# The first part's square sums at the end of a feed-forward block, moved beside the block's last products

## What is computed

```python
f1 = swiglu(rms_norm(x, ffn1_pre_g[l]), ffn1_w_gate[l], ffn1_w_up[l], ffn1_w_down[l])
x = x + FFN_RESIDUAL_WEIGHT * rms_norm(f1, ffn1_post_g[l])
m = token_mixer(rms_norm(x, mix_pre_g[l]), w_in[l], ...)
...
f2 = swiglu(rms_norm(x, ffn2_pre_g[l]), ffn2_w_gate[l], ffn2_w_up[l], ffn2_w_down[l])
x = x + FFN_RESIDUAL_WEIGHT * rms_norm(f2, ffn2_post_g[l])
```

## Time and profile before

| | us |
|---|---|
| median of 3 runs | 4127.95 |
| lowest, highest run | 4118.88, 4129.35 |
| the profiled execution's own time | 4127.35 |
| its span, first to last instruction | 4125.6 |
| PE busy in the span | 3960.3 |
| DVE busy | 1906.0 |
| ACT busy, POOL busy | 1408.2, 1416.1 |

### The profile page before, as it was taken

The page is one execution under the profiler, slowest core; times in us unless marked ns, Lnnn a source line. Parts: engine busy times, 40 slices in busy tenths (PEclk is TensorE's granted clock), DMA queues, the critical chain, the costliest instruction groups (busy, mean ns, idle before and its releaser), DMA issues.

```text
span 4125.6 us, 49381 instructions
## 1 busy us (share of the span) xinstructions
PE 3960.3 (96%) x20616; PEld 3199.7 (78%) x20616; DVE 1906.0 (46%) x2819; ACT 1408.2 (34%) x2256; POOL 1416.1 (34%) x849
## 2 busy tenths in 40 slices
PE   7999999999999999999999999999988999999988
PEld 5888888666565556888888789999967998888867
DVE  3323223533344535232232477654387526666654
ACT  3111111433333334111111354331253336666663
POOL 2222323133443452223232224432262123434364
PEclk9999999999999999999999999999999999999989
DMA  2111111110000021111111101121112220000014
GB/s 93 51 41 51 52 41 57 61 43 21 21 21 21 16 83 56 42 51 52 41 57 46 36 31 42 52 98 50 61 36 82 95 62 28 26 28 28 23 63 136
DMA packets 57807, 206.08 MB, mean 50 GB/s; under 512 B 7344, under 2 KB 10992, under 8 KB 57200
## 3 DMA queue, kind: packets, MB, share of 16 engines
q1 hardware_dynamic: 45744, 158.55, 11.7%
q0 software_dynamic: 9280, 41.75, 2.7%
q10 hardware_dynamic: 2560, 2.61, 0.2%
HBM read 177.40 MB, written 25.49 MB: 49 GB/s over the span
## 4 chain that ended last, share of the span: by engine, by line
PE 78%; DVE 12%; ACT 4%; POOL 3%; issue 1%; DMA 0%; DVEq 0%; ACTq 0%
PE ps L395 15%; PE ps L396 15%; PE ps L397 15%; PE ps L3509 4%; PE ps L3441 2%; PE ps L3443 2%; PE ps L3442 2%; PE ps L1354 2%; PE ps L1356 2%; PE ps L1355 2%; PE ps L3493 2%; POOL wlo L369 2%; PE ps L3539 2%; PE ps L546 2%; PE ps L1454 2%; PE ps L1425 1%
## 5 line engine op out<-in xcount | busy, mean ns | idle before, releaser
L369 POOL TENSOR_TENSOR wlo<-raw,whi 128x1024 fp32r<-128x1024 f32 x286 | 690.1, 2423 | 832.5 <-ACT whi L360 832.2
L395 PE MATMUL ps<-fxh,whi 128*128 128x512 f32 x1488 | 605.1, 407 | 41.6 <-POOL wlo L369 19.3
L396 PE MATMUL ps<-fxh,wlo 128*128 128x512 f32 x1488 | 582.1, 391 | 0.0
L397 PE MATMUL ps<-fxl,whi 128*128 128x512 f32 x1488 | 581.2, 391 | 0.0
L395 PE MATMUL ps<-xh,whi 128*128 128x352 f32 (+1 forms) x1400 | 473.5, 338 | 11.8 <-DVE sxin L2662 5.1
L396 PE MATMUL ps<-xh,wlo 128*128 128x352 f32 (+1 forms) x1400 | 450.7, 322 | 0.0
L397 PE MATMUL ps<-xl,whi 128*128 128x352 f32 (+1 forms) x1400 | 450.0, 321 | 0.0
L360 ACT ACTIVATE whi<-raw 128x1024 fp32r<-128x1024 f32 x286 | 294.8, 1049 | 451.9 <-PE ps L397 383.5
L395 PEld LDWEIGHTS ps<-fxh,whi 128*128 128x128 f32 x1488 | 280.7, 189 | 121.2 <-issue 35.8
L805 POOL TENSOR_TENSOR hl<-t,hh 128x512 fp32r<-128x512 f32 x88 | 114.0, 1295 | 733.1 <-ACT hh L750 733.1
L396 PEld LDWEIGHTS ps<-fxh,wlo 128*128 128x128 f32 x1488 | 280.9, 189 | 67.9 <-issue 12.1
(11 more groups left out here) (424 smaller groups left out, 7812.1 us busy)
## 6 DMA issues: line engine op xcount, KB each, us to landing
raw<-in_w_dram SPq DMA_DIRECT2D x286, 512.0 KB, 3.3
rs_scratch<-res POOLq DMA_DIRECT2D x2, 4160.0 KB, 14.0
res<-rs_scratch POOLq DMA_DIRECT2D x8, 520.0 KB, 5.1
szin<-zs_scratch SPq DMA_DIRECT2D x8, 520.0 KB, 3.2
gs_scratch<-oot POOLq DMA_DIRECT2D x8, 520.0 KB, 5.9
res<-rs_scratch POOLq DMA_DIRECT2D x2, 1408.0 KB, 6.7
og<-gs_scratch POOLq DMA_DIRECT2D x16, 176.0 KB, 2.6
oot<-rs_scratch POOLq DMA_DIRECT2D x2, 1408.0 KB, 9.1
```

What stands on the lines that cost most here:

```text
L369: pool.x.tensor_tensor(K.wlo[n % 3][:, :], K.raw[n % 2][:, :], K.whi[n % 3][:, :], ALU.subtract).then_inc(*S.up("w_lo", n))
L395: pe.x.matmul(out, wh, xh, start=k == 0, stop=False)
L396: pe.x.matmul(out, wl, xh, start=False, stop=False)
L397: last = pe.x.matmul(out, wh, xl, start=False, stop=k == K - 1)
```

## The change

At both ends the stage 0 squares of part a are summed behind groups 2 to 7 of the first pass (rows 0 to 5, in a new method `ahead`) and behind groups 0 and 1 of the second (rows 6 and 7), one at a time. DVE takes a's mean at group 1 of the second pass and its root at group 3, and applies rows 0 to 3 beside groups 4 to 7, with the rests of rows 0 to 2. Of part b's squares PE sums five behind the pass and the other three within the next product, behind rows 1 to 3. ACT's order follows: b's last three squares stand between a's rounded rows, and the next weight unit is rounded behind a's row 3 rather than ahead of row 0. Part b's mean and root stand at a's rows 5 and 7 on DVE rather than at 3 and 5. The arithmetic is the same.

```diff
-def pe_paced(pe, L, st):
+def pe_paced(pe, L, st, other=None):
     def wait(k):
         pe.wait_ge("late_lo", (L.tag, k))
         if st and k:
             pe_square(pe, L, 1, k - 1)
+            if other and k < 4:
+                pe_square(pe, other, 0, k + 4)
@@ pe_ffn
         down_group(10, 0, ft, wh, wl)
+        after.ahead(ft)
@@ new
+def act_two_norms(act, a, b, unit):
+    for k in range(8):
+        act_square(act, a, 0, k)
+        if k == 3:
+            act_units(act, unit)
+    act_root(act, a, 0)
+    for k in range(5):
+        act_square(act, b, 0, k)
+    for k in range(8):
+        act_high(act, a, k)
+        act_square(act, a, 1, k)
+        if k < 3:
+            act_square(act, b, 0, k + 5)
+        if k == 3:
+            act_units(act, unit + 1)
+        if k == 5:
+            act_root(act, b, 0)
+def dve_two_norms_beside(dve, a, ft):
+    if ft == 1:
+        dve_variance(dve, a, 0)
+    elif ft == 3:
+        dve_root(dve, a, 0)
+    elif ft >= 4:
+        dve_apply(dve, a, ft - 4)
+        if ft > 4:
+            dve_low(dve, a, ft - 5)
+def dve_two_norms_end(dve, a, b):
+    for k in range(4, 8):
+        dve_apply(dve, a, k)
+        dve_low(dve, a, k - 1)
+        if k == 5:
+            dve_variance(dve, b, 0)
+        if k == 7:
+            dve_root(dve, b, 0)
+    dve_low(dve, a, 7)
@@ IntoMixerPE, IntoEvenPE
+    def ahead(self, ft):
+        if ft >= 2:
+            pe_square(self.pe, self.norms[0], 0, ft - 2)
     def beside(self, ft):
-        if ft < 4:
-            pe_square(self.pe, self.norms[0], 0, 2 * ft)
-            pe_square(self.pe, self.norms[0], 0, 2 * ft + 1)
+        if ft < 2:
+            pe_square(self.pe, self.norms[0], 0, ft + 6)
     def end(self):
-        for k in range(8):
+        for k in range(5):
             pe_square(self.pe, self.norms[1], 0, k)
```

More of the change, by code:

```diff
@@ L873, in end @@
         act, (a, b) = self.act, self.norms
[L874 to L885, removed]
+        act_two_norms(act, a, b, UNIT_AT["IN.24"])
         act_units(act, UNIT_AT["IN.24"] + 2)
@@ L902, in beside @@
     def beside(self, ft):
[L903 to L906, removed]
+        dve_two_norms_beside(self.dve, self.norms[0], ft)
     def end(self):
         dve, (a, b) = self.dve, self.norms
[L910 to L918, removed]
+        dve_two_norms_end(dve, a, b)
         for k in range(8):
@@ L977, in end @@
         act, (a, b, d) = self.act, self.norms
[L978 to L989, removed]
+        act_two_norms(act, a, b, UNIT_AT["E.0"])
         act_units(act, UNIT_AT["E.8"])
@@ L1339, in gate @@
         pe.bank(c)
-        pe_product(pe, K.bank(c), 8, eight1(K, wh, wl, c0, c1), ("gate", c), pe_paced(pe, norms[c], 1))
+        pe_product(pe, K.bank(c), 8, eight1(K, wh, wl, c0, c1), ("gate", c), pe_paced(pe, norms[c], 1, None if c else norms[1]))
         pe_square(pe, norms[c], 1, 7)
@@ L2049, in first @@
                 pe_product(pe, K.bank(b, c1 - c0), 8, eight(K, wh, wl, c0, c1), (name, c),
-                           pe_paced(pe, norms[c], name == "E.0"))
+                           pe_paced(pe, norms[c], name == "E.0", None if c else norms[1]))
                 pe.banks[b] = [freed[name](c)]
```

## The result

The changed kernel takes 4141.41 us (median of 9 runs, 4137.53 to 4146.12), the kernel before beside it 4129.23 (9 runs, 4118.88 to 4133.94). The ratio is 1.0034, 95% interval 1.0025 to 1.0042: slower by 12 us by the medians. The forecast was 4134.0, in a range of 4123 to 4141. The profiled execution took 4146.08 us, one of the longer of the nine.

The account below looks back on a forecast made before the run. PE was taken to bound both first passes, DVE the rows behind them. First end 2.2, second end 0.4 and clock 3.4 summed to +6.0 us; against the median of 4127.95 that gave 4134.0 us, range 4123 to 4141.

Parts of the forecast that it names:

- The two passes: At both ends PE waits for ACT's first square, 2.2 and 2.05 us; the passes end 1.4 and 1.3 us later.
- DVE's start and the chain behind it: First end: DVE's first rest 3.9 us earlier, but delays behind it make +2.2 us; second end +0.4 us.
- half of a stretch's loss: Expected sign at the first end: DVE's first rest near 779.3 plus half of the 1.7 us a low-clock stretch loses.
- Rows 2 and 3: Part a's rows at the first end, waiting on ACT: 0.4 and 1.05 us late, 1.5 us in the sum.
- The moved unit: The weight unit's POOL part falls between DVE's rows and holds one instruction, 2.88 us rather than 0.75: 2.1 us.
- The clock: PE's new wait in each first pass brings one stretch at 0.5 of the clock, 1.7 us each, 3.4 us together.
- twelve waits: PE's waits of 2.1 to 2.9 us up to 2400 us before; behind eleven the granted clock fell to 0.5.
- Sum: Both ends and the clock: 2.2 + 0.4 + 3.4 = +6.0 us, 4134.0 us, with nothing behind either end giving it back.
- The first (the start is kept): Rival: at both ends DVE's earlier start is kept and PE's clock holds in the first passes; 4124.0 us, chance 0.17.
- The second: Rival: longer low-clock stretches in both first passes, another ahead of the mixer's first projections; 4141.5 us, chance 0.08.
- The third: Rival: at the second end POOL's weight rest starts before a's last rest, PE 2.4 us later; 4136.4 us, chance 0.15.

Follow-up runs that it names:

- e8: Changed kernel with PE's squares of part a one group later in both first passes, extra discarded PE products filling the scan's waits: 4130.56 us, ratio 1.0005.
- e9: Changed kernel with ACT's rounding of the second weight unit moved behind part b's third square, scan's waits filled with discarded PE products: 4131.66 us, ratio 1.0005.
- e14: The change at the first end alone, second end as in the kernel before, the scan's DVE/POOL order fixed by a wait: 4131.29 us, ratio 1.0008.
- e1: Changed kernel profiled once more, nothing edited: 4147.58 us (one execution).
- e3: Changed kernel with extra discarded PE products ahead of the scan's waits for DVE: 4133.84 us, ratio 1.0004.
- e7: The change at the first end alone, second end as in the kernel before, scan's waits filled with discarded PE products: 4135.82 us, ratio 1.0013.
- e13: Kernel before with an added POOL wait in the scan that puts DVE first of the pair: 4128.30 us, ratio 0.9997.
- e5: Changed kernel with an added POOL wait in the scan at block 1 that puts DVE first of the pair: 4136.03 us, ratio 1.0019.
- e10: Changed kernel with ACT's rounded rows one ahead of part b's squares, scan's waits filled with discarded PE products: 4128.54 us, ratio 1.0000.
- e11: Changed kernel with squares a group later, rounded rows one ahead and the scan's DVE/POOL order fixed, nothing filled: 4123.70 us, ratio 0.9986.
- e2: Kernel before profiled once more, nothing edited: 4127.13 us (one execution).
- e6: Kernel before with an added DVE wait in the scan at block 1 that puts POOL first of the pair: 4136.38 us, ratio 1.0026.

## Why the prediction was wrong

- **The two passes: right.** Waits of 2.2 and 2.05 us for ACT's first square were forecast, 2.07 and 1.92 measured. e8 removes them and what hangs on them.
- **DVE's start and the chain behind it: right where it can be read.** The first rest was forecast near 779.3 plus half of a stretch's loss (0.85), in a trace that begins 1.2 us later, so at 781.4. It came at 782.38: it bears the whole loss of 1.7 us and not half of it. Rows 2 and 3 were to be 0.4 and 1.05 late: DVE's waits are 0.57 and 1.17. The moved unit was to hold one instruction for 2.1: 2.85 us in place of 0.75, and e9 gives 2.0 back at the second end. The first end was to cost 2.2 + 1.7 = 3.9 and cost 4.5 (4.4 in e14, 4.0 in e1); the second 0.4 + 1.7 = 2.1 and cost 2.2 in the first profile and 0.6 to 0.7 in the others with the change's own order, which have no stretch in its first pass. Together that is 6.7 us in the first profile and 4.6 in e1.
- **The clock: right in kind, its count too high.** The wait in the first pass of the first end was followed by a stretch in 5 of 8 traces that have it, that of the second end in 1 of 8 (it is 1.92 us in all). I had taken one each. That is 1.7 x 5/8 + 1.7 x 1/8 = 1.3 us rather than 3.4. But where the first did not come, a stretch of 6.8 us came at 803 in two of three (e3 and e7), and the end was the longer for it (81.5 us). The sum also left out what the change takes away: PE's waits of 2.22 us at 784.09 and 2.72 at 2357.20, which in the trace of before are followed by stretches of 6.8 and 3.4 us, are gone after, and the stretches with them. What they cost isn't measured; PE goes at DVE's pace there. Of the twelve waits that were counted before, two, at 1459.31 and 1462.94, share one stretch, so there are ten stretches and not eleven. And one short stretch more or less is 4132.3 to 4135.7; 4130.5 is two less.
- **The step that failed, in the paragraph "Sum": "Nothing behind either end gives it back: DVE's mean at 825.21 and its root at 2421.51 lead into the next stage's chain."** I asked whether later slack gives something back, and not whether a later stage costs more when it is reached at another moment. It does: the scan went from 119.35 to 132.1 and 132.2 us in the two profiles of the changed kernel, through the order of two instructions that start within 0.15 us of each other. The prediction's sum had nothing for it. With the order fixed the kernel takes 4136.0, 5.4 us less and 2 us from the forecast, and the ratio's interval for it, 1.0010 to 1.0028, holds the sum of 6.0 us.
- **Rivals.** The first (the start is kept) did not occur. The second named the third 3 us wait of PE, ahead of the mixer's projections (2.98 at 806.12, as it said), but of the traces with the change's own order there only e3 and e7 have that stretch, and no first pass has a stretch longer than 3.4 us. That its 4141.5 us meets the measured 4141.41 is luck. The third did not occur: a's last rest at 2376.00 took 0.58 us, and POOL's came behind it.
- **What could have been seen.** The trace of before has the pair: POOL at 3010.56 stretched to 2.02 us, DVE 0.15 us ahead of it. One could have told that the order hangs on little, but not which way a shift of 7 us turns it.

## What to carry to other kernels

Check a cost that is worked out at one place against the trace at that place, and only then the total: here the sum of 6.0 us stands beside 6.7 and 4.6 in two traces where it was made, and the total was twice as large. If two traces differ behind a stage that the edit doesn't touch, look for the first pair of instructions on DVE and POOL that have changed places; if one wait fixes their order, write it, since it costs nothing where the order was already so (e13) and took 5.4 of the 12.2 us of loss where it wasn't (e5). When sums are moved from one pass into another, the queue that feeds them has to be laid out anew: with the rounded rows taken out from behind the squares that wait for a tile, the loss in the median was gone (e10), and with the first square a group later as well there was a gain (e11).

## What was not expected of the hardware

- Where the two instructions of the pair overlap, the later one is stretched, by 0.97 us (POOL, 2.02 for 1.05) or by 0.80 (DVE, 2.07 for 1.27). The Trainium skill, page SBUF — State Buffer, section "Who interferes with whom", has the later to issue block; both rows agree with it. That the choice between the two is worth 12.8 us of a loop in a profiled execution is what these traces add.
- The scan's head is in a stretch of 17 us at 0.5 of the clock, which starts at another point of the program from one execution to the next: 3.4 us after the first product in e2, 1.9 in e6, while the instructions up to its end keep their times. The same instructions behind it thereby come earlier by different amounts, 0.16 us on DVE and 0.35 on POOL.
- The same wait of PE, 2.07 us at the same instruction, is followed by a stretch at 0.5 of the clock (1.2 GHz) in five traces and by full clock (2.4 GHz) in three. In the scan three waits of 2.97 us are followed by such a stretch and a fourth is not, in both traces of the changed kernel.
